# Gate projections as seven block products over feature pairs, input halves and token halves

## What is computed

```
h = rmsnorm(x, g_attn);  proj = h @ w_in
u, q_lat, kv_lat, k_pe, q_mem, g_logit = split(proj)
br_a = S5 state space scan of u, GELU, gated linear unit
br_b = latent attention (8 heads);  br_c = cross attention into 256 memory tokens (4 heads)
gates = sigmoid(g_logit).reshape(b, l, 3, 1024)
merged = gates[0] * br_a + gates[1] * br_b + gates[2] * br_c
x = x + merged @ w_out
x = x + hierarchical_moe(rmsnorm(x, g_ffn))     # 32 experts, 96 MB of weights
```

## Time and profile before

| | us |
|---|---|
| median of 3 runs | 635.71 (635.5 to 635.72) |
| the profiled execution | 637.16 |
| its span in the profile | 635.3 |
| TensorE busy in the span | 611.6 (96%) |
| VectorE busy | 291.2 (46%) |
| ScalarE busy | 186.6 (29%) |
| GpSimd busy | 148.7 (23%) |

### The profile page before, as it was taken

The page is one execution under the profiler, slowest core; times in us unless marked ns, Lnnn a source line. Parts: engine busy times, 40 slices in busy tenths (PEclk is TensorE's granted clock), DMA queues, the critical chain, the costliest instruction groups (busy, mean ns, idle before and its releaser), DMA issues.

```text
span 635.3 us, 9981 instructions
## 1 busy us (share of the span) xinstructions
PE 611.6 (96%) x3746; PEld 378.6 (60%) x3746; DVE 291.2 (46%) x813; ACT 186.6 (29%) x582; POOL 148.7 (23%) x341
## 2 busy tenths in 40 slices
PE   8999999999999999999999999999999999978895
PEld 7888867677456667666677767854443444333341
DVE  3343947757883589772043321685123133132112
ACT  5534224532478445423100101211221221111111
POOL 1596627733584525510000000000000000000000
PEclk9999999999899999999999999999999999989899
DMA  8893553212301343323589990099999999999993
GB/s 285 193 292 113 191 171 100 68 67 85 113 2 33 117 150 100 100 67 100 150 251 401 406 387 24 14 411 401 421 419 420 420 419 419 421 419 419 422 391 98
DMA packets 57715, 150.57 MB, mean 237 GB/s; under 512 B 12352, under 2 KB 40448, under 8 KB 45760
## 3 DMA queue, kind: packets, MB, share of 16 engines
q1 hardware_dynamic: 57664, 149.89, 63.4%
HBM read 147.12 MB, written 2.76 MB: 236 GB/s over the span
## 4 chain that ended last, share of the span: by engine, by line
PE 91%; DVE 3%; DMA 2%; issue 2%; ACT 1%; SPq 0%; DVEq 0%
PE PS L832 28%; PE PS L842 21%; PE PS L1229 10%; PE PS L1123 7%; PE PS L1268 6%; PE PS L1258 5%; PE PS L958 2%; PE PS L915 2%; PE PS L1180 2%; PE PS L983 2%; PE PS L825 1%; PE PS L1025 1%; PE PS L966 1%; DMA W<-in_w_in 1%; PE PS L904 1%
## 5 line engine op out<-in xcount | busy, mean ns | idle before, releaser
L832 PE MATMUL PS<-hT,W 128*128 128x320 f32 x416 | 117.2, 435 | 0.0
L832 PEld LDWEIGHTS PS<-hT,W 128*128 128x128 f32 x416 | 77.5, 190 | 33.4 <-issue 3.8
L1229 PE MATMUL PS<-E,xT 128*32 128x256 f32 (+1 forms) x1088 | 64.5, 390 | 7.7 <-issue 7.4
L1229 PEld LDWEIGHTS PS<-E,xT 128*32 128x32 f32 x1088 | 35.5, 112 | 36.1 <-issue 16.2
L2206 POOL TENSOR_SCALAR means<-sums 128x4 f32<-128x4 f32 (+3 forms) x35 | 7.3, 210 | 188.6 <-ACT junk L1368 187.6
L1123 PE MATMUL PS<-h,S 128*128 128x512 f32 (+1 forms) x96 | 48.2, 625 | 0.3 <-DVE S L1996 0.3
L842 PE MATMUL PS<-W,hT 128*128 128x256 f32 (+5 forms) x256 | 41.7, 353 | 0.0
L1268 PE MATMUL PS<-yb,WG 128*128 128x512 f32 (+1 forms) x96 | 38.5, 609 | 0.8 <-DVE yb L2121 0.8
L842 PEld LDWEIGHTS PS<-W,hT 128*128 128x128 f32 (+1 forms) x256 | 31.5, 163 | 8.4 <-issue 1.3
L842 PE MATMUL PS<-W,mergedT 128*128 128x384 f32 (+3 forms) x192 | 35.7, 381 | 0.0
L832 PE MATMUL PS<-uT,W 128*128 128x320 f32 x128 | 34.6, 432 | 0.0
(11 more groups left out here) (316 smaller groups left out, 985.3 us busy)
## 6 DMA issues: line engine op xcount, KB each, us to landing
E<-in_w_e SPq DMA_DIRECT2D x93, 1024.0 KB, 22.3
W<-in_w_in SPq DMA_DIRECT2D x7, 1536.0 KB, 7.2
W<-in_w_in SPq DMA_DIRECT2D x7, 1024.0 KB, 8.0
W<-in_w_mem_kv SPq DMA_DIRECT2D x4, 1024.0 KB, 6.9
W<-in_w_glu SPq DMA_DIRECT2D x4, 768.0 KB, 7.5
W<-in_w_out SPq DMA_DIRECT2D x2, 1536.0 KB, 14.8
X<-in_x_prompt SPq DMA_DIRECT2D x4, 512.0 KB, 4.8
W<-in_w_o_mem SPq DMA_DIRECT2D x1, 1536.0 KB, 6.7
```

What stands on the lines that cost most here:

```text
L832: ins = mm(out[:, 0:TOK], w[:, k, cols:cols + 128], rhs[:, k, :], start=(k == 0), stop=(k == kt - 1))
L1229: ins = mm(PS[r:r + B, AB, 128 * which.start:128 * which.stop], xT[:, k, place_ + B * n:place_ + B * n + B], E13[slot][:, which, k, j::2], ...
```

## The change

Each branch's 8 gate units of 128 features become 4 pairs of 256. For a pair the weights are four blocks (input half r, feature tile c): a11, a12 (second input half, first tile), a21 (first half, second tile), a22. The tokens of `hT` are four blocks b11, b12, b21, b22 (input half, 160 tokens). In place of eight block products there are seven, of sums of blocks (Strassen, in Winograd's form). Token sums t1 to t4 are made once on GpSimd (`token_sums`), weight sums s1, s2 and a21 for each pair on GpSimd (`weight_sums`) and a12 - s2 on VectorE. A pair is three PSUM units: `a` (three products), `b` and `c` (two each). VectorE adds them into the gate's place, and ScalarE applies tanh to 640 columns after `c`. Chunks hold two gates (1 MB) and leave place in their slot for s1, s2. `fill_up` puts the parts by estimated work. `qT` moves to another place and the reload of X behind the last gate, as the token sums lie where X goes.

```diff
-over_d("gateC", KD, 128, (1, 2, 0))
+over_d("gateC", KD, 128, (1, 2, 0, 1))
...
-        "gateC": 4.3, "gateB": 4.3, "gateA": 4.3, "outC": 2.1, "outB": 2.1, "kq": 1.8, "mem": 0.8, "mla": 0.8}
+        "outC": 2.1, "outB": 2.1, "kq": 1.8, "mem": 0.8, "mla": 0.8}
+GATE_WORK = {"a": 3.2, "b": 2.2, "c": 2.2}
+FILL = 4.3
...
+    def fill_up():
+
+        nonlocal room
+        room += FILL
+        while fills and room >= work_of(fills[0]) / 2:
+            room -= work_of(fills[0])
+            fill()
...
-    fills = [("gateB", d) for d in range(KD)] + [("gateA", d) for d in range(KD)]
-    held, pace, due = False, LATE_PACE, spent
-    attention("mla", MLA_UNITS, 1)
+    fills = gates("B") + gates("A")
+    held, pace, due, room = False, LATE_PACE, spent, 0.0
+    attention("mla", MLA_UNITS)
...
-    return "dve" if unit[0].startswith("out") else "act"
+    return "dve" if unit[0].startswith(("out", "gate")) else "act"
...
-            sp.wait_ge(s["psum_full"], UNIT_NO["mla", "S", len(MLA_UNITS) - 1] + 1)
+            sp.wait_ge(s["psum_full"], UNIT_NO["gateA", GATE_PAIRS - 1, "c"] + 1)
...
+                def product(n, lhs, rhs):
+                    for k in range(KD // 2):
+                        ins = mm(out[:, HALF * n:HALF * n + HALF], lhs[:, k, :], rhs[:, k, :], start=(k == 0), stop=(k == KD // 2 - 1))
+                    return ins
+
+                if part == "a":
+                    product(0, a11, b11)
+                    product(1, a12, b21)
+                    pe.wait_ge(s["x_sums"], 4)
+                    pe.wait_ge(s["early_sums"], no + 1)
+                    end(product(2, s2, sumT[:, 1]))
+                elif part == "b":
+                    product(0, s1, sumT[:, 0])
+                    end(product(1, a21, sumT[:, 2]))
...
+                    product(1, a22, sumT[:, 3])
+                    pe.wait_ge(s["late_sums"], no + 1)
+                    end(product(0, a12, b22))
...
-                    empty(dst[:, which[0], :], full((kind, which[0]))[:, 0:TOK], ACT.Tanh, scale=0.5)
+                    m, part = which
+                    if part == "c":
+                        act.wait_ge(*emptied_at(UNIT_NO[kind, m, "c"]))
+                        z = {"A": gateA, "B": gateB, "C": mergedT}[kind[-1]][:, 2 * m:2 * m + 2, :]
+                        fn(z, z, ACT.Tanh, scale=0.5).then_inc(s["gates_made"], 1)
...
+                if part == "a":
+                    _, a12, _, _, _, s2 = gate_blocks(f"{kind}{m}")
+                    link(V_.tensor_copy(z[:, 3], src[:, 0]))
+                    joined["a"] = st.mark(V_.tensor_tensor(z[:, 0::3], z[:, 3:4].broadcast_to([128, 2, HALF]), src[:, 1:3], ALU.add),
+                                          s["emptied_dve"])
+                    V_.tensor_tensor(a12, a12, s2, ALU.subtract).then_inc(s["late_sums"], 1)
+                elif part == "b":
+                    st.after(joined["a"])
+                    link(V_.tensor_tensor(z[:, 1:3], z[:, 3:4].broadcast_to([128, 2, HALF]), src[:, 0:2], ALU.add))
+                    joined["b"] = st.mark(V_.tensor_tensor(z[:, 3], z[:, 2], src[:, 0], ALU.add), s["emptied_dve"])
+                else:
+                    st.after(joined["b"])
+                    st.mark(V_.tensor_tensor(z[:, 1:3], z[:, 1:3], src[:, 0:2], ALU.add), s["emptied_dve"])
...
+            def token_sums():
...
+                first = st.mark(tt(t1, b12, b11, ALU.subtract), s["x_sums"])
+                st.mark(tt(t3, b22, b12, ALU.subtract), s["x_sums"])
+                st.after(first)
+                link(tt(t2, b22, t1, ALU.subtract), s["x_sums"])
+                st.mark(tt(t4, b21, t2, ALU.subtract), s["x_sums"])
...
+            def weight_sums(no):
...
+                link(tt(s1, a21, a22, ALU.add))
+                link(tt(s2, s1, a11, ALU.subtract))
+                tt(a21, a11, a21, ALU.subtract).then_inc(s["early_sums"], 1)
```

115 lines of the change are left out of this document (79 added, 36 removed).

## The result

The changed kernel takes 669.06 us (median of 4 runs, 667.77 to 670.12), beside 635.72 for the kernel before: a ratio of 1.0509, 95% interval 1.0484 to 1.0533. It is slower, as forecast, but by 33 us where 5.6 were forecast, and outside the range of 630 to 649.

A forecast was written before the change was run, and what follows sets the result against it. TensorE sets the time, but VectorE would bind in the MLA stretch: 97.8 us plus 5 shared cost from turn 9 at 221.0 puts outB at 323.8, 5.6 later; added to 635.71 that is 641.3 us, range 630 to 649.

The forecast's parts named there:

- the products: Gate matmuls on TensorE: 56 instructions a pair at 0.136 us, 0.99 us less a pair, 11.9 us over 12 pairs.
- the MLA stretch without contention: From the turn's start to outB: 97.8 us with VectorE holding up TensorE, before any shared cost.
- The forecast 5.2 us for the bank of a score unit: MLA stretch, ahead of unit c of pair 2: TensorE stands 5.2 us until ScalarE frees score unit 4's bank.
- the second wait of 1.9 us: MLA stretch: TensorE waits 1.9 us more for the bank that VectorE frees by emptying unit b of pair 3.
- the shared cost: MLA stretch: GpSimd's sums stretch VectorE's operations with two SBUF inputs, 5 us for three pairs, bounds 0 and 11.
- the gate C stretch: 113 to 166 us: the chain into the latents ends within 1 us of before; put at 0, from -0.7 to +2.
- the token sums and GpSimd's queue: GpSimd's four token sums take 6 us; its queue holds them between the turn tables, costed at nothing.
- Ahead of the gated linear unit's first weights: Three more loads and the state stores delay these weights about 4 us; covered, cost nothing, without cover up to 4 us.
- every microsecond at outB moves the end by as much: From the first outB unit to the end: any delay or gain at outB carries over in full.
- the key stretch: Turn 9 and the second y move out of it: 1.9 us less there, the same coming back later.
- The signs: Expected in the profile: TensorE gaps ahead of a unit c and the query latents, VectorE above 90% busy 222 to 262 us.
- Rival (3): Whole kernel slower by more: late chunks or sums, waits lowering TensorE's clock, or slow loads; 650 to 665 us, chance 0.06.

The follow-up runs named there:

- e7: As e6, but the last two pairs, gateA.2 and gateA.3, by the seven products, with their sums: 642.82 us, 1.0097 against the kernel before.
- e15: Changed kernel, all twelve pairs by seven products, weight sums and joins on 8 columns, no token sums, x fetched early: 637.68 us, 1.0022 against the kernel before.
- e1: Changed kernel with GpSimd's three weight sums a pair on 8 columns instead of 512: 645.67 us, 1.0149 against the kernel before.
- e14: Changed kernel with VectorE's joins kept, weight sums on 8 columns, no token sums, x fetched early: 642.85 us, 1.0122 against the kernel before.
- e2: Changed kernel with VectorE's joins and a12 subtraction on 8 columns, GpSimd's sums whole: 661.73 us, 1.0402 against the kernel before.
- e3: Changed kernel with the edits of e1 and e2 together, neither weight sums nor joins: 641.25 us, 1.0081 against the kernel before.
- e4: Changed kernel with the planner's gate costs raised so that turns are spaced as before: 668.33 us, 1.0505 against the kernel before.
- e12: Changed kernel with the first two weight sums of each pair issued twice, 60 sums instead of 36: 681.71 us, 1.0720 against the kernel before.
- e6: Changed kernel's chunks, slots and late x fetch, but all 12 pairs by plain products, no sums: 642.11 us, 1.0083 against the kernel before.
- e9: As e6, but x fetched early again, behind the last MLA score unit: 637.25 us, 1.0007 against the kernel before.

## Why the prediction was wrong in size

**Right: the products.** The step gave 0.136 us an instruction and 0.99 us a pair. The 24 instructions above start over 3.36 us (307.75 less 304.39), 0.140 each, and e7 gained 2.0 us on two pairs. The mean duration is 301 ns in e15, as forecast; in the changed kernel it is 314 and 324, with the slow clock in it. The weight loads of 160-column matmuls did overlap.

**Right: the MLA stretch without contention.** I forecast 97.8 us from the turn's start to outB; from the first score, 1.1 us earlier, that is 98.9. e1, which has joins and no weight sums, took 97.9 (322.1 less 224.2), e14 97.9 as well, the kernel before 96.6. The forecast 5.2 us for the bank of a score unit is e1's longest wait, 4.6 us for ScalarE's P. This queue argument held within a microsecond or so for the first wait, and the unit behind it starts 36.5 us after turn 9's first product, forecast 37.1. That the whole stretch fits is in part luck: the second wait of 1.9 us didn't come, and the gates took 64.8 us in place of 61.0, as the clock stood low behind the first.

**Wrong, and most of the error: the shared cost, +5 us.** The count of pairs was wrong: "so three pairs give 3 x 3.8 x 0.47". I counted only the pairs up to score unit 4 in the MLA stretch, because I held that afterwards "TensorE has the longer queue", and I put the gate C stretch at 0 without its own sums. The loss of the sums (after less e1, by the moments in their traces) is 8.6 us in the gate C stretch, 13.8 in the MLA stretch and 0.5 in the keys; at the start there is 1.6 us more, but that is the clock of that execution and not the weight sums, as e2 with all its sums starts like e1. Of the 13.8 us, 6.9 stand ahead of unit c of pair 2 (43.4 us from turn 9's first product to it, 36.5 in e1), which is what I gave 5 us, and 6.9 behind it (67.2 us from it to outB, 60.4 in e1), which I gave nothing. VectorE never came free: each pair brings its sums again, and 73.51 of 85 us are busy there. All twelve pairs at my own rate give 21.4 us, where the runs give 22.9. My bound of 11 was the whole sum time of three pairs and had the same mistake.

That the rate of 1.8 us a pair fits is half right and half luck. VectorE is held up as priced: its busy time is 349.7 us, without the weight sums 327.6 (e1), so 22.1 us or 1.8 a pair. But I took what VectorE loses for what TensorE loses. TensorE stood 12.8 us more, and about 14 us more went to the slow clock behind its waits, for which my sum had no term at all.

**Wrong: the gate C stretch, which I put at 0, from -0.7 to +2.** It came out at +8.5 us. In e1 it is 0.0 and in e14 +0.7, as the chain said, so the chain was right and the sums were left out of it. The five stretched instructions at 134 us stand in this stretch, and so does a wait of 4.8 us for ScalarE's P.

**Wrong: the token sums and GpSimd's queue, "I cost the queue itself at nothing".** The four sums take 6.2 us beside VectorE's norm products and cost 3.6 us, half as a wait and half as slower matmuls behind it, or 1.9 where the clock didn't drop. I named what stood behind them (the tables) and missed VectorE beside them.

**Wrong: "Ahead of the gated linear unit's first weights ... covered. Cost nothing; without cover up to 4 us".** It cost 4.8 us by itself. What I looked at was not what was late: w_glu was in time, and w_out, some 50 us later, was not.

**Wrong: every microsecond at outB moves the end by as much.** 28.4 at outB became 32.6 at the end, by the wait on w_out (2.4 us) and its slow matmuls (the first 64 start over 20.65 us, 18.93 before).

**Wrong: the key stretch, -1.9.** It took 1.3 us more than before. A turn and a y went out of it, but TensorE stood for KQ in their place (1.8 us in e1, e2, e3, e14 and e15 alike). That is 1.8 of the 3.2 us between forecast and result; the rest is open.

**The signs.** TensorE's gap ahead of unit c stands where it was named. VectorE is busy for 76% of the window from 222 to 262 us and not for over 90, but the stretch meant had moved: from 234.6 to 275.6 it is 92%. TensorE also waits 2.4 us ahead of the query latents, as named, but at 171.8 us.

Rival (3), with 650 to 665 us and a chance of 0.06, was the nearest. It named waits that lower the clock, which was about half of the truth, but its price was still too low and the late sums and loads that it named first were small.

## What to carry to other kernels

Work given to GpSimd is not free because GpSimd is idle. Against VectorE instructions with two SBUF inputs it cost about half of its duration here (0.64 us for sums of 1.37), for every sum in the whole kernel and not only in the tightest stretch; compare with VectorE doing it, which here was cheaper. A wait of the engine that sets the time has a second price, the clock behind it. Multiplications saved on TensorE count only where nothing else in the same loop is within their size of binding; two pairs of twelve kept their gain in the trace here, though not visibly in the time, and even all twelve without a single sum gained nothing. Before moving a load later, ask whether the DMA engines are full there, and look at the transfers behind it and not only at the next one.

## What I had not expected of the hardware

A short wait of TensorE can be paid about twice. After 1.85 us of waiting, 64 instructions took 15.77 us in place of 14.08; after 3.38 us, 21.91 in place of 19.10; after 5.52 us, instructions of 160 columns started 0.28 us apart (8 in 2.26 us) in place of 0.136, which is the 1.2 GHz level. Or it is paid once: after the same wait at the same place (1.85 us in e1, 1.75 in e2, 1.88 in e4, 1.76 in e12) the same 64 instructions took 14.08 us. Which of the two happens differed between executions, and no run here shows what decides it. The mean granted clock is 0.963 in the changed kernel and 0.991 before. The clock adds chance elsewhere too: e6 and e9 do the same up to outB, yet e6 has the first MLA score at 219.8 and e9 at 221.4; the kernel before shows a clock of 0.97 in its key stretch (166 to 221 us) and e6 shows 1.00. So a microsecond or two between two traces is not yet an effect of an edit.
